# A one-layer decoder kernel: gates and output copies reordered, the compression's end and the samples' selection regrouped

## Time and profile before

| | |
|---|---|
| Median of 3 runs | 2539.79 us (2538.99 to 2541.76) |
| The profiled execution: its own time | 2543.22 us |
| The profiled execution: its span | 2541.6 us |
| PE busy / weight loads | 94% / 86% of the span |
| DVE, ACT, POOL busy | 48%, 32%, 13% |
| Mean granted TensorE clock | 0.965 of full speed |

### The profile page before, as it was taken

One profiled execution on the slowest core, in us unless ns is written; L12 is line 12 of the kernel. 1 busy time (PEld: TensorE's weight loads), 2 busy tenths in 40 slices (PEclk: granted clock), 3 DMA queues, 4 the chain that ended last, 5 costly groups with the idle time before them and its releaser, 6 DMA issues. The chain is left out here.

```text
span 2541.6 us, 40409 instructions
## 1 busy us (share of the span) xinstructions
PE 2392.3 (94%) x15386; PEld 2180.1 (86%) x15386; DVE 1216.2 (48%) x2160; ACT 813.7 (32%) x1783; POOL 321.1 (13%) x570
## 2 busy tenths in 40 slices
PE   6998898999877999889899999999999999999999
PEld 6977797999766889745699999977999999999997
DVE  4457776304657777566622233334343433333334
ACT  5354364444435665323412121222211111111110
POOL 1004221011204322355100000000000000000000
PEclk9988698999999999889999999999999999999999
DMA  4011543231110000177311122130211111111111
GB/s 151 26 34 47 147 129 104 68 109 26 43 36 1 1 1 18 40 188 189 87 38 50 38 51 83 38 117 16 68 50 50 50 35 50 50 50 34 50 34 67
DMA packets 216413, 156.77 MB, mean 62 GB/s; under 512 B 76339, under 2 KB 197350, under 8 KB 216165
## 3 DMA queue, kind: packets, MB, share of 16 engines
q1 hardware_dynamic: 186708, 121.96, 17.1%
q0 software_dynamic: 8160, 19.08, 2.9%
q10 hardware_dynamic: 21360, 13.22, 1.8%
HBM read 142.76 MB, written 15.59 MB: 62 GB/s over the span
## 5 line engine op out<-in xcount | busy, mean ns | idle before, releaser
L177 PE MATMUL ps<-brT_r,ff_wih 128*128 128x344 f32 x1008 | 322.0, 319 | 0.0
L179 PE MATMUL ps<-brT_r,ff_wi_r 128*128 128x344 f32 x1008 | 321.6, 319 | 0.0
L178 PE MATMUL ps<-xnT_r,ff_wih 128*128 128x344 f32 x1008 | 321.3, 319 | 0.0
L3798 ACT ACTIVATE ff_sa<-ps 128x344 f32<-128x344 f32 x66 | 30.3, 459 | 563.4 <-PE ps L179 563.3
L177 PEld LDWEIGHTS ps<-brT_r,ff_wih 128*128 128x128 f32 x1008 | 189.6, 188 | 1.0
L179 PEld LDWEIGHTS ps<-brT_r,ff_wi_r 128*128 128x128 f32 x1008 | 189.4, 188 | 0.0
L177 PE MATMUL ps<-x_r,mg_wh 128*128 128x344 f32 x576 | 185.1, 321 | 4.6 <-DVE xnT_r L165 4.6
L178 PEld LDWEIGHTS ps<-xnT_r,ff_wih 128*128 128x128 f32 x1008 | 189.0, 187 | 0.4
L178 PE MATMUL ps<-xnT_r,mg_wh 128*128 128x344 f32 x576 | 184.4, 320 | 0.0
L3834 DVE TENSOR_TENSOR x<-x,ps 128x512 f32<-128x512 f32 (+1 forms) x198 | 134.9, 686 | 100.8 <-PE ps L179 100.1
L179 PE MATMUL ps<-x_r,mg_w_r 128*128 128x344 f32 x552 | 176.2, 319 | 0.0
(11 more groups left out here) (618 smaller groups left out, 5878.2 us busy)
## 6 DMA issues: line engine op xcount, KB each, us to landing
ff_wi<-in_w_ffn_in SPq DMA_DIRECT2D x42, 512.0 KB, 5.1
mg_w<-in_w_in SPq DMA_DIRECT2D x23, 512.0 KB, 4.1
ff_wo<-in_w_ffn_out SPq DMA_DIRECT2D x11, 1024.0 KB, 5.0
s_pages<-in_cache_kv_slc POOLq DMA_DIRECT2D x128, 64.0 KB, 3.0
s_pages<-in_cache_kv_slc SPq DMA_DIRECT2D x128, 64.0 KB, 3.0
sc_X<-in_cache_kv_cmp SPq DMA_DIRECT2D x56, 128.0 KB
sc_X<-in_cache_kv_cmp POOLq DMA_DIRECT2D x56, 128.0 KB, 2.4
mg_w<-in_w_branch SPq DMA_DIRECT2D x23, 256.0 KB, 4.5
```

The lines of the kernel that those rows point to most:

```text
L177: nc.tensor.matmul(out, wh, xh, start=(first and k == 0), stop=False)
L178: nc.tensor.matmul(out, wh, xl, start=False, stop=False)
L179: ins = nc.tensor.matmul(out, wl, xh, start=False, stop=(last and k == n - 1))
L3798: nc.scalar.activation(sa[:, s % 2, :], ps[:, s % 2, 0:BLK], ACT.Silu).then_inc(silued, 1)
```

## The change

In the mLSTM, the gates use four banks, PE's tile n waits for gate n-4, and DVE's order is average(7), gate 0, norm(6), norm(7), gates 1 to 7. In the compression, project waits for each gelu alone, turn_k of the first part stands between two eighths of the last sample, the remaining half of the first token tile is split there too, and the last store of keys is moved to the token projection's start, where ACT waits for it at its fifth span, with spans cut at tiles 0, 1, 3, 5, 8. In the prompt's attention ACT copies a tile's turned output ahead of the turned probabilities. In the samples, prep and select are one block. Its small loads go out on ACT's queue, PE's overlap product goes ahead of the values, and the new keys' products and the turning of units 0 and 1 move there from the attend block.

```diff
@@ -849,10 +849,13 @@
...
-                    if n >= 2:
-                        pe.wait_ge(gated, n - 1)
+                    if n == 2:
...
+                        pe.wait_ge(interk, N)
+                    if n >= 4:
+                        pe.wait_ge(gated, n - 3)
                     for a in range(4):
-                        ins = nc.tensor.transpose(ps[:, n % 2, a * P:(a + 1) * P],
+                        ins = nc.tensor.transpose(ps[:, n % 4, a * P:(a + 1) * P],
                                                   Htm[:, h, 4 * half + a, :], c("ident"))
...
@@ -987,12 +990,12 @@
...
+                average(NCK - 1)
+                gate(0)
                 norm(NCK - 2)
-                average(NCK - 1)
-                for n in range(4):
-                    gate(n)
                 norm(NCK - 1)
-                for n in range(4, 8):
+                for n in range(1, 8):
                     gate(n)
...
-        starts = (0, 1, 4, 8)
+        starts = (0, 1, 3, 5, 8)
...
+                sp.dma_start(M["kc_kept"][:, 12 * NCS:], brT[0:HD, :, :].rearrange("p k t -> p (k t)")[
+                    :, 12 * NCS:B * G * NCS]).then_inc(M["spilled"], 16)
...
-                        if g == 0 and t in starts:
-                            pe.wait_ge(x_low, 2 * starts.index(t) + 1)
+                        if g == 0 and t in starts[1:]:
+                            pe.wait_ge(x_low, 2 * starts.index(t))
...
-                    if i == 0:
+                    if i < 2:
...
-                    if i == 1:
+                    if i == 5:
...
@@ -2076,10 +2082,11 @@
...
                         exponentials(u + 1)
...
+                    if u % (2 * H) == 2 and u > 2 * H:
+                        out(act, u // (2 * H) - 1)
                     for m in range(first_item[u], first_item[u + 1]):
                         keep(nc.scalar, m, u)
-                    if u % (2 * H) == 2 and u > 2 * H:
-                        out(act, u // (2 * H) - 1)
                 out(act, QT - 1)
...
-def stage_s_prep(M, A):
...
@@ -2549,10 +2518,7 @@
...
-                sp.wait_ge(kdone, 4)
-                sp.dma_start(M["kc_kept"][:, EARLY * NCS:],
-                             kcT[:, EARLY:, :].rearrange("p n q -> p (n q)")).then_inc(M["spilled"], 16)
-                sp.wait_ge(stored, 48)
+                sp.wait_ge(stored, 32)
...
-                    pe.wait_ge(activated, 2 * b + 2)
...
                     for cc in range(2):
+                        pe.wait_ge(activated, 2 * b + cc + 1)
...
-                pe.wait_ge(knorm, 1)
-                turn_k(0, EARLY)
+                        if e == 5 and b == B - 1:
+                            pe.wait_ge(knorm, 1)
+                            turn_k(0, EARLY)
                 project(B - 1)
...
+                act.wait_ge(knorm, 1)
+                act.wait_ge(kc_out, 16)
+                high(nc, x_hi0, x_in0).then_inc(M["tok_high"], 1)
...
                         next_low(0)
+                        dve.wait_ge(M["tok_high"], 3)
+                        low(nc, x_lo, x_in, x_hi).then_inc(tok_low, 1)
...
-                dve.wait_ge(M["tok_high"], 3)
-                low(nc, x_lo, x_in, x_hi).then_inc(tok_low, 1)
                 keep_k(EARLY // 4)
+                dve.wait_ge(M["tok_high"], 4)
+                low(nc, x_lo0, x_in0, x_hi0).then_inc(tok_low, 1)
...
         with st.block() as block:
...
-                kv = M["kvS"].rearrange("b (r c d) -> b r c d", c=2, d=HD)
-                for b in range(B):
-                    q = 32 * (b // 2)
-                    sp.dma_start(A["vrow"][q:q + 1, b % 2, :, :], kv[b:b + 1, :, 1, :]).then_inc(vrows, 16)
...
-                load_win(sp, M["I"]["cache_kv_win"], A["rows0"], 0, A["in_win"][0])
-                load_mem(sp, M["I"]["cache_kv_mem"], A["rows0"], 0, A["in_mem"][0])
+                sp.dma_start(A["pt"][:, :], I["page_table"].rearrange("b n -> (b n)").unsqueeze(0)).then_inc(A["pt_in"], 16)
                 sp.wait_ge(A["pt_in"], 16)
-                load_kinds(sp, M["I"]["cache_kv_slc"], A["pages"], A["pt"], 0, 0, A["in_k"][0], A["in_v"][0])
...
+                load_kinds(sp, I["cache_kv_slc"], A["pages"], A["pt"], 0, 0, A["in_k"][0], A["in_v"][0])
...
             def _(pe):
...
+                ins.then_inc(q_turned, 1)
                 pe.wait_ge(M["kept_in"], 32)
+                pe.wait_ge(q_kept, 1)
...
+                pe.wait_ge(summed, 1)
+                nc.tensor.matmul(ps[0:B * G, 3, 0:NB], pg[:, :], c("overlap")[0:NCS, :],
+                                 start=True, stop=True).then_inc(weighed, 1)
...
                 pe.wait_ge(pkept, 1)
...
                 ins.then_inc(attended, 1)
...
+                pe.wait_ge(q_kept, 2)
+                for br in range(2):
...
+                        nc.tensor.matmul(ps[0:H, 7, br * B + b:br * B + b + 1], A["qz"][:, b, :],
...
+                for f in range(3):
...
+                        pe.wait_ge(A["in_win"][0], 64)
...
+                        pe.wait_ge(A["in_mem"][0], 16)
...
+                    for a in range(4):
+                        ins = nc.tensor.transpose(ps[:, f, a * P:(a + 1) * P], at[:, a * 256:a * 256 + P], c("ident"))
+                    ins.then_inc(k_turned, 1)
                 pe.wait_ge(ranked, 1)
                 for b in range(B):
                     ins = nc.tensor.matmul(ps[0:H, 6, b * NB:(b + 1) * NB], c("expand")[0:B * G, b * H:(b + 1) * H],
...
             @block.scalar
...
+                load_win(act, I["cache_kv_win"], A["rows0"], 0, A["in_win"][0])
+                load_mem(act, I["cache_kv_mem"], A["rows0"], 0, A["in_mem"][0])
...
+                    act.dma_start(A["vrow"][q:q + 1, b % 2, :, :], kv[b:b + 1, :, 1, :]).then_inc(vrows, 16)
                 act.wait_ge(maxed, 1)
...
+                act.wait_ge(attended, 1)
...
+                    nc.scalar.activation(dst, ps[:, f, :], ACT.Copy).then_inc(k_kept, 1)
+                act.wait_ge(vrows, 16 * B)
+                act.wait_ge(k_kept, 3)
...
-                dve.wait_ge(attended, 2)
+                dve.wait_ge(weighed, 1)
...
+                dve.wait_ge(attended, 1)
...
@@ -3042,15 +3075,8 @@
...
-                        ins = nc.tensor.matmul(ps[0:H, 7, br * B + b:br * B + b + 1], qz[:, b, :],
-                                               knT[:, br, b:b + 1], start=True, stop=True)
-                ins.then_inc(first, 1)
-                turn(0)
                 for u in range(NU):
-                    if u + 1 < NU:
+                    if 2 <= u + 1 < NU:
                         turn(u + 1)
                     scores(u)
 
...
```

More of the change, by code:

```diff
@@ L2435, in load_pages, with key_places @@
+def key_places(M):
+    flat = M["x2"][:, :, :].rearrange("p t d -> p (t d)")
+    return [flat[:, q * 2048:(q + 1) * 2048] for q in range(2)]
 def load_pages(eng, cache, dst, pt, b, half, done):
@@ L2775, in stage_s_select @@
                              "attended", "summed", "ranked", "spread", "tri_ok"))
-        vrows = sem("vrows")
+        vrows, q_turned, q_kept, weighed, k_turned, k_kept = (
+            sem(n) for n in ("vrows", "q_turned", "q_kept", "weighed", "k_turned", "k_kept"))
         chain = Chain(sem("step"))
@@ L2894, in stage_s_attend @@
         rows = [A["rows0"], flat[:, 4096:8192].rearrange("p (k n) -> p k n", k=2)]
-        kTb = [flat[:, q * 2048:(q + 1) * 2048] for q in range(2)]
+        kTb = key_places(M)
+        DONE = fill0[2]
         s_ = st.sb("s", [H, 2, LEN])
@@ L2935, in keep @@
             j = f - fill0[u]
-            eng.wait_ge(turned, f + 1)
+            eng.wait_ge(turned, f + 1 - DONE)
             if u >= 2:
@@ L3097, in _ @@
                 load_mem(act, I["cache_kv_mem"], rows[1], 1, in_mem[1])
-                for f in range(fill0[1]):
-                    if f % 2 == 0:
-                        keep(act, f)
                 for u in range(NU):
@@ L3172, in use @@
                                                        ALU.mult, ALU.add).then_inc(used, 1)
-                dve.wait_ge(first, 1)
                 nc.vector.tensor_copy(snew[:, :, :].rearrange("p r b -> p (r b)"), ps[0:H, 7, 0:2 * B]).then_inc(newk, 1)
                 dve.wait_ge(newk, 1)
-                for f in range(fill0[1]):
-                    if f % 2 == 1:
-                        keep(dve, f)
                 for u in range(NU):
-                    if u + 1 < NU:
+                    if 2 <= u + 1 < NU:
                         for f in range(fill0[u + 1], fill0[u + 2]):
```

123 lines of the change are left out of this document (58 added, 65 removed).

## The result

The changed kernel takes 2518.3 us in the median of 4 runs (2514.2 to 2518.5), beside 2540.8 for the kernel before on the same chip: a ratio of 0.9905, with a 95% interval of 0.9893 to 0.9916. The forecast was 2519.2 us with a range of 2513 to 2527. The profiled execution after took 2518.48 us with a span of 2516.9, so the two spans lie 24.7 us apart.

A forecast was written before the change was run, and what follows sets the result against it. PE, busy for 94% of the span, was taken to bound the kernel. Terms of 3.2 + 0 + 2.9 + 5.3 + 6.8 + 2.4 = 20.6 us, off the 2539.79 median, gave 2519.2 us, range 2513 to 2527.

The forecast's parts named there:

- mLSTM tail: At the mLSTM's end, reordered gates and norms save 3.2 us, the middle of 2.8 and 3.6.
- seven gates of 1.61 / 2 = 0.81: At the mLSTM's end, DVE's seven gates behind the last norm take 0.81 us each, ending at 238.7.
- Compression's end: At the end of the compression, moved turns and copies cancel out: 0 us, between -0.3 and +0.3.
- Token projection's start: PE's first token tile starts with its block, without waiting for store, ACT and DVE: 2.9 us, bounds 2.3 and 3.0.
- Output copies: In the prompt's attention, ACT's earlier copy removes PE's waits: 5.3 us saved, bounds 3.2 and 6.4.
- discount of 1.1 for early query tiles: In the prompt's attention, early query tiles have less room as the exponential ends late: 5.3 kept of 6.4 us.
- six waits hold 6.4: In the prompt's attention, PE waits 6.4 us in six places for ACT's copy of a turned output.
- The softmax loop: Rival in the prompt's attention: DVE and ACT's loop takes the copies' 5.3 us back, giving 2524.5 us; chance 0.07.
- Prep and select in one block: In the samples, the joined block ends with DVE's chain and attend starts 6.8 us earlier, bounds 5.5 and 7.3.
- Attend's start: At the attend block's opening, 3.6 us of PE's work leave; with the low clock 2.4 us saved, between 1.8 and 5.2.
- The rival with the clock up early: PE's work in select raises the clock before attend: 5.2 us saved there instead of 2.4, giving 2516.4; chance 0.16.
- such a gain would show me wrong: Sign against the forecast, anywhere in the kernel: a gain in a stretch that the diff leaves alone; no size given.

The follow-up runs named there:

- experiment 3: Changed kernel with the mLSTM's gates over two banks: in the old order 2525.0 us, ratio 0.993; in the new order 2520.4 us, ratio 0.9907.
- experiment 4: Changed kernel with the compression's end and the token projection's start as before the change: 2519.4 us, ratio 0.9913.
- experiment 2: Changed kernel with ACT's output copy put back behind the copies of turned probabilities: 2527.0 us, ratio 0.9942.
- experiment 6: Changed kernel with the select block's thirteen small loads issued by SP again, none by ACT: 2524.0 us, ratio 0.9923.
- experiment 7: Changed kernel with PE's overlap product put back behind the multiplication with the values: 2523.0 us, ratio 0.9918.
- experiment 8: Changed kernel with the new keys' products and turning and copying of units 0 and 1 back in the attend block: 2522.6 us, ratio 0.9912.
- experiment 5: Changed kernel with prep, select and attend as three blocks again, as before the change: 2529.5 us, ratio 0.9949.
- experiment 1: The changed kernel run again, unedited: 2520.1 us, ratio 0.9913 to the kernel before.
- experiment 9: Changed kernel with unused turns of the identity matrix added on PE where it waits, in select, attend's end and merge: 2523.5 us, ratio 0.9922.
- experiment 10: Changed kernel with the ranking in three wide operations instead of five: 2515.4 us, ratio 0.990; the same plus short added identity turns on PE: 2516.1 us, ratio 0.9888.

## Why the prediction was right, and where it wasn't

**mLSTM tail, 3.2 forecast, 3.9 shown** (3.7 by experiment 3), above the upper bound of 3.6. The step that failed is "seven gates of 1.61 / 2 = 0.81": the second gate of that pair had waited for PE's turns. Unpaced a gate takes 0.67, so seven take 4.70 and not 5.6, and the same sum gives 3.8. The path of roots and norms was right (norm(7) ended 2.9 us behind POOL's start, 3.0 forecast). The upper bound went by PE's 0.98 us for four turns; PE took 3.48 for the sixteen, 0.87 each, stayed ahead and bounded nothing.

**Compression's end, 0 forecast.** Experiment 4 has a loss of 0.4 to 0.7, but less than the segment's scatter; nothing is shown against the 0.

**Token projection's start, 2.9 forecast, 2.8 shown** by experiment 4 and by the first product, 0.05 behind the block's start instead of 2.85. The segment's other 2.1 us are the clock's: behind the first product it stayed at 0.50 for 5.9 us before and for 3.8 after, and later in the segment it was at 0.50 for 6.8 us before and 3.4 after:

```profile
656.00:664.00 8.00, 6.59 (x28) 5.93 (x29) 4.89 (x5) 1.98 (x6) 2.63 (x2) 0.57 0.02 4
```

```profile
646.00:654.00 8.00, 6.34 (x35) 5.71 (x36) 5.87 (x7) 2.24 (x8) 2.88 (x2) 0.79 0.02 4
```

**Output copies, 5.3 forecast, 7.5 shown**, above the bound of 6.4. The discount of 1.1 for early query tiles was right: the first two copies kept 0.9 us of wait. The step that failed is "six waits hold 6.4", in two ways: a seventh wait of 1.05 stood behind a copy too, under DVE's name, and each stop that went took 0.14 to 0.26 us of PE's busy time with it, 1.0 in sum (experiment 2). The softmax loop took nothing back: PE's other waits are the same to 0.1 us.

**Prep and select in one block, 6.8 forecast, 7.5 shown** up to the block's start (22.9 against 30.4), 0.2 above the bound of 7.3. Its steps held: the overlap product was worth 3.5 (3.0 forecast), DVE and not SP ended the block, and with SP's loads kept it would have been SP (experiments 6 and 7). A third chain, POOL's with its DRAIN, wasn't in the forecast; it ended 0.4 us ahead of DVE's, so that it cost nothing here was luck.

**Attend's start, 2.4 forecast.** The 3.6 us of work are gone, and 0.4 came back up to the last turn of keys, so 3.2; by experiment 8, 2.4. The rival with the clock up early came half true: the clock was at 1.00 from 1058.2, then fell to 0.57 for 1065 to 1069. The moved turns, a part of the cause that it gave, weren't needed for the rise, as experiment 8 shows. The Trainium skill ("TensorE: Matmul & The Clock Gate", Part 1) has the clock throttled by default and released by activity. The rise at 1058.2 in the changed kernel, after 4 us of products and ahead of the moved turns, agrees with that, and so do those of experiments 5 and 8, at 1062.4 and 1062.5; in the kernel before, the same 3.58 us of products with the values left it at 0.50. The fall comes behind 5 us in which PE was busy for 2.18.

**The sum.** The diff's own effects by segments are 3.9 + 0 + 2.8 + 7.5 + 11.2 = 25.4 us up to the attend block's first score, where I had 20.6 with attend's start in it. The gain was 24.7 between the profiled spans, 22.5 between the medians and 22.8 in experiment 1, so my sum was 2 to 4 us short, by the terms above. That the median, 2518.3, lies 0.9 us from the forecast is luck in part: against the forecast's terms the shown ones are 0.7 + 0 - 0.1 + 2.2 + 0.7 + 0.8 = 4.3 us larger, and losses to the clock and the scatter of the medians hid some two of them; the kernel before, from whose median of 2539.79 I subtracted, has 2540.78 with one run more. The clock's share cancelled: about 4 us were gained in stretches whose code the diff leaves alone or whose own effect is taken off above (1.4 up to the chunks' end, 2.1 in the token projection, some 0.6 in the samples and the compression, the last within that segment's scatter), and 4.8 lost in the attend block and behind it. I had said that such a gain would show me wrong. It shows that a term was missing: where the granted clock falls in stages whose instructions don't change, which came to 4 to 5 us in either direction here.

That missing term is seen best where no instruction differs. At the start of the mLSTM stage PE is idle for 3.4 us in both kernels. Before the change the clock fell in that gap:

```profile
138.00:140.00 2.00, 0.73 (x5) 0.45 (x3) 1.24 (x2) 0.46 (x1) 0.00 (x0) 1.00 0.00 0
140.00:142.00 2.00, 0.00 (x0) 0.00 (x0) 1.80 (x1) 0.00 (x0) 0.00 (x0) 0.67 0.00 0
142.00:144.00 2.00, 1.88 (x4) 1.20 (x5) 1.59 (x2) 1.90 (x2) 0.16 (x1) 0.50 0.14 9
```

and after it, it did not:

```profile
140.00:142.00 2.00, 0.25 (x1) 0.28 (x2) 1.67 (x2) 0.28 (x1) 0.16 (x1) 1.00 0.00 0
142.00:144.00 2.00, 2.00 (x8) 1.31 (x8) 1.73 (x2) 1.99 (x2) 0.00 (x0) 1.00 0.17 9
```

All code up to there is the same in all fourteen profiles. In nine of them the clock fell in that gap (before, and experiments 3 with the new order, 5 to 9 and both of 10), in two it fell 1 to 2 us behind it (3 with the old order, and 4), and in three it didn't (after, and experiments 1 and 2). So this part of the gain isn't the change's. At the attend block's end and the merge's start it went the other way. Before, the clock fell once, while PE was idle, and was back soon:

```profile
1244.00:1250.00 6.00, 3.61 (x25) 1.62 (x24) 2.20 (x5) 0.18 (x1) 0.00 (x0) 1.00 0.00 0
1250.00:1254.00 4.00, 0.51 (x2) 0.54 (x3) 2.29 (x9) 1.89 (x6) 0.00 (x0) 0.50 0.18 26
1254.00:1256.00 2.00, 2.00 (x9) 1.89 (x8) 1.77 (x4) 2.00 (x3) 0.00 (x0) 0.50 1.15 330
1256.00:1258.00 2.00, 1.15 (x5) 0.86 (x3) 1.99 (x2) 2.00 (x3) 0.00 (x0) 0.79 1.14 279
```

After the change it fell twice, from 1211.8 to 1215.2 with PE busy all along, and again from 1222.1 to 1235.7:

```profile
1212.00:1215.00 3.00, 3.00 (x16) 1.93 (x15) 0.00 (x0) 0.00 (x0) 0.00 (x0) 0.50 0.00 0
...
1226.00:1230.00 4.00, 3.34 (x12) 3.26 (x12) 3.75 (x7) 4.00 (x7) 0.00 (x0) 0.50 0.96 240
1230.00:1235.00 5.00, 4.09 (x15) 3.65 (x15) 5.00 (x4) 5.00 (x5) 0.00 (x0) 0.50 0.47 123
```

That is 3.4 us of PE's work at half speed in the first place (1.9 lost in the segment), and 8.7 in the second, where before there were 3.3: 2.5 lost. The same page of the Trainium skill says that the chip's measure of activity runs on its own and isn't aligned with the kernel's start. The traces agree as far as they can: the same gap is followed by a fall in one kernel and not in the other, and the first low stretch of all began at 33.3 to 36.4 us in the fourteen profiles, with all code ahead of both the same. Against it, experiment 1 repeats the changed kernel's low stretches within 0.7 us, which may be chance. That experiments 2, 4, 7 and 10 lose none of the 2 us at the attend block's end, at other start times, fits it too. What exactly decides whether a gap brings a fall, and whether the change itself has a part in where the falls behind it lie, no run here shows.

## What to carry to other kernels

A row that groups several instructions holds their pacing: take the duration of one from a place where it doesn't wait. Judge a change of a few microseconds by segments between the same instructions in both traces, not by the total: here edits worth 2.8 and 7.5 us in their segments showed as no loss and 2.1 in the span of one profile. But don't take that one span for the kernel either: by the medians of five runs the second was worth 7.4. When several engines issue and compute towards a block's end, removing the last one pays only up to the next (5.1 us for SP's loads; 0.4 for a ranking made 2.6 shorter), and an engine's end includes its DRAIN, which a timeline doesn't show. A wait is named by what came last, so look for the other waits at the same instruction before you count them.

## What was not expected of the hardware

The granted clock can fall while PE is busy: in the changed kernel it fell at 1211.8, where PE had been busy for 5.26 of the 5.8 us before, and it was at 0.50 from 1212 to 1215 with PE busy for 3.00 of 3 us. What PE did there and just before was turns 8 columns wide and products with 8 columns of weights. The same work kept 1.00 in experiments 2, 4, 7 and 10.

With the order of instructions nearly unchanged, the attend block took 128.0 to 130.7 us, its end 27.2 to 29.2 and the rest 1291.6 to 1294.3 in the profiles without added turns in them, by where these falls came.

A stop of PE costs more than its idle time, by 0.14 to 0.26 us each here (experiment 2). And POOL's DRAIN ended 2.3 to 3.6 us behind its last page load, which held up one block (experiment 10).
